# Prompt attention of a hybrid decoder step on one Trainium2 core: score tiles of up to 1024 keys cut into units of at most 512, and the setup's loads in another order

## What is computed

```python
def diff_attend(q, k, v, q_pos, k_pos, lam):
    s = jnp.einsum('ntkgch,nskch->nkgcts', q, k, preferred_element_type=jnp.float32) * SCALE
    mask = k_pos[None, :] <= q_pos[:, None]
    s = jnp.where(mask, s, -jnp.inf)
    p = jax.nn.softmax(s, axis=-1)
    a = p[:, :, :, 0] - lam * p[:, :, :, 1]
    return jnp.einsum('nkgts,nskv->ntkgv', a, v.astype(jnp.float32))
```

## Time and profile before

| | |
|---|---|
| median of the executions | 2490.93 us |
| the profiled execution | 2487.62 us, its span 2485.8 us |
| busy in the span | PE 87%, PEld 80%, DVE 46%, ACT 39%, POOL 51% |
| mean granted TensorE clock | 0.912 of full |
| setup, to the first instruction of the next block | 0 to 50.6 us |
| prompt attention | about 1482 to 2080 us |

### The profile page before, as it was taken

One profiled execution on the slowest core, in us unless ns is written; L12 is line 12 of the kernel. 1 busy time (PEld: TensorE's weight loads), 2 busy tenths in 40 slices (PEclk: granted clock), 3 DMA queues, 4 the chain that ended last, 5 costly groups with the idle time before them and its releaser, 6 DMA issues. The chain is left out here.

```text
span 2485.8 us, 37618 instructions
## 1 busy us (share of the span) xinstructions
PE 2170.9 (87%) x13193; PEld 1995.5 (80%) x13193; DVE 1155.8 (46%) x1914; ACT 971.2 (39%) x1572; POOL 1279.6 (51%) x682
## 2 busy tenths in 40 slices
PE   4999999999279998999889987877777787898998
PEld 4999999999279998999889985655665666666998
DVE  3698889889845003222100005555555554346101
ACT  4455555555444112111121125555555554234111
POOL 2799999999733324433311125555455552224232
PEclk7999999999669999999989987888888887997999
DMA  6112111121223222223222230000000005882221
GB/s 234 51 54 65 60 60 60 48 63 53 84 60 122 69 94 88 69 77 94 90 82 95 86 128 26 18 26 18 17 26 17 9 1 155 255 262 76 60 77 70
DMA packets 182037, 192.51 MB, mean 77 GB/s; under 512 B 11435, under 2 KB 147060, under 8 KB 181332
## 3 DMA queue, kind: packets, MB, share of 16 engines
q1 hardware_dynamic: 181952, 191.48, 24.4%
HBM read 145.52 MB, written 47.63 MB: 78 GB/s over the span
## 5 line engine op out<-in xcount | busy, mean ns | idle before, releaser
L222 POOL TENSOR_TENSOR w_lo<-w_raw,w_hi 128x1024 fp32r<-128x1024 f32 x116 | 279.6, 2411 | 603.3 <-ACT w_hi L218 603.3
L242 PE MATMUL ps<-Hhi,w_hi 128*128 128x352 f32 x1704 | 560.5, 329 | 18.3 <-POOL w_lo L222 11.7
L242 PE MATMUL ps<-Hhi,w_lo 128*128 128x352 f32 x1704 | 550.9, 323 | 0.0
L242 PE MATMUL ps<-Hlo,w_hi 128*128 128x352 f32 x1704 | 549.9, 323 | 0.0
L777 DVE SCALAR_TENSOR_TENSOR ps<-U,dww,ps 128x512 f32<-128x512 f32 x608 | 403.1, 748 | 0.0
L218 ACT ACTIVATE w_hi<-w_raw 128x1024 fp32r<-128x1024 f32 x116 | 122.1, 1053 | 665.7 <-PE ps L242 244.6
L696 POOL TENSOR_TENSOR pool_acc<-pool_acc,prod 128x1024 f32<-128x1024 f32 x144 | 346.3, 2405 | 31.0 <-ACT prod L645 22.7
L242 PEld LDWEIGHTS ps<-Hhi,w_hi 128*128 128x128 f32 x1704 | 321.9, 189 | 27.9 <-POOL w_lo L222 18.4
L242 PEld LDWEIGHTS ps<-Hlo,w_hi 128*128 128x128 f32 x1704 | 323.1, 190 | 2.1
L242 PEld LDWEIGHTS ps<-Hhi,w_lo 128*128 128x128 f32 x1704 | 322.1, 189 | 0.0
L645 ACT ACTIVATE prod<-U,dww 128x1024 f32<-128x1024 f32 x176 | 197.0, 1147 | 249.8 <-POOL pool_acc L696 143.3
(11 more groups left out here) (237 smaller groups left out, 3876.4 us busy)
## 6 DMA issues: line engine op xcount, KB each, us to landing
w_raw<-conv_w_in SPq DMA_DIRECT2D x48, 512.0 KB, 4.1
w_raw<-attn_w_in SPq DMA_DIRECT2D x40, 512.0 KB, 4.7
kpage<-cache_k SPq DMA_DIRECT2D x64, 256.0 KB, 3.0
vpage<-cache_v SPq DMA_DIRECT2D x64, 256.0 KB
res<-Y SPq DMA_DIRECT2D x2, 4224.0 KB, 21.4
gate<-sg SPq DMA_DIRECT2D x16, 528.0 KB, 4.0
sgl<-gate SPq DMA_DIRECT2D x16, 528.0 KB, 3.7
xres<-res SPq DMA_DIRECT2D x16, 528.0 KB, 3.9
```

What stands on the lines that cost most here:

```text
L222: pool.tensor_tensor(wlo[s][:, :, :], raw[s][:, :, :], whi[s][:, :, :].bitcast(F32), ALU.subtract).then_inc(w_lo, 1)
L242: mm = pe.matmul(ps[:, 3 * dst + c, 0:CH], w[:, k, :], r(k)[:, c * CH:(c + 1) * CH], start=start and k == 0 and w is whi[s] and r is rhs_h ...
```

## The change

Attention: the tiles with i >= 4 are cut into two units, one of 512 keys and one of the rest, so that a head has 12 units (4 narrow tiles, then 4 x 2) in place of 8 tiles. A unit never takes more than one bank for each softmax, the bank pairs alternate by unit, and the scores of unit u wait for the exps of unit u - 2. The two units of a wide tile have maxima of their own: the second unit's exps use the joint minimum of the negated maxima (`run_done`), ACT makes two weights that bring the first unit to the same maximum, DVE joins the sums, POOL scales three pieces and then adds. `LAG` goes from 2 tiles to 5 units; on DVE the maxes now stand ahead of the coefficients. Products of small statistics are written as reductions over adjacent columns of `stats`, with one operand, in place of `tensor_tensor`. `p0` gets eight buffers and `p1` four. `v_hi` moves from behind `hi` to ahead of it, `q_hi` from i = 4 to the unit with y % 12 = 1.

Setup: the weight tiles are loaded last of the small loads; `st_in` is loaded only when the norm's roots are made; the spreading of the norms comes ahead of `dwin` and lambda; the state is transposed in the next block, behind the first `unit_by_tile`; the wait for the write of `res` moves there too. Five semaphores cover the nine input loads.

```diff
     (setup, SP)
-                for s, kind in ((0, 0), (1, 1)):
-                    sp.dma_start(raw[s][:, :, :], conv_src(0, kind)).then_inc(raw_in[s], 16)
...
-                sp.dma_start(dwin[:, :], a["conv_dw_w"][0]).then_inc(dw_in, 16)
                 for i, name in enumerate(("attn_lambda_q1", "attn_lambda_k1", "attn_lambda_q2", "attn_lambda_k2")):
                     sp.dma_start(lamv[:, i, :], a[name]).then_inc(lam_in, 16)
+                sp.dma_start(dwin[:, :], a["conv_dw_w"][0]).then_inc(dw_in, 16)
                 sp.dma_start(ptab[:, :], a["page_table"].rearrange("(o b) p -> o (b p)", o=1)).then_inc(lam_in, 16)
-                sp.dma_start(stg[:, :, :], st_src).then_inc(st_loaded, 16)
-
+                for s, kind in ((0, 0), (1, 1)):
+                    sp.dma_start(raw[s][:, :, :], conv_src(0, kind)).then_inc(raw_in[s], 16)
                 sp.wait_ge(xe_act, NXT)
                 sp.wait_ge(xe_dve, NXT)
+                sp.wait_ge(Norm.std_ready, 1)
+                sp.dma_start(stg[:, :, :], st_src).then_inc(st_loaded, 16)
                 sp.dma_start(res_d[0], Y[:, :, :]).then_inc(res_out[0], 16)
-                sp.wait_ge(res_out[0], 16)
     (next block: PE; ACT and DVE copy the state out and wait for res_out)
+                        unit_by_tile(pe, n, e, e, norms[0])
+                        if first and s == 0:
+                            turn_state()
     (attention)
+        LAG = 5
+        UNITS = 12
+        VALUES = {10: (0, (0,)), 11: (0, (1, 2)), 12: (0, (3,)),
+                  17: (1, (0, 1)), 18: (1, (2, 3)), 19: (1, (4, 5)), 20: (1, (6, 7))}
+        OUTPUTS, TOTALS, SUMS = {13: 0, 21: 1}, {14: 0, 22: 1}, {15: 0, 23: 1}
+        NEW_VALUES, NEXT_Q = 9, 1
...
+        def score_ap(x, n, c):
+            return ps[:, 2 * (unit_of(x, n) % 2) + c, 0:width(x, n)]
     (PE scores)
+                    if u >= 2:
+                        pe.wait_ge(exp_done, 2 * NU * g + 2 * (u - 2) + 2)
     (ACT)
+                def exp(g, x, n, c):
+                    if n == 0:
+                        act.wait_ge(mx_done, 2 * NU * g + 2 * unit_of(x, n) + c + 1)
+                    else:
+                        act.wait_ge(run_done, 4 * GH * g + wides(x) + 1)
...
+                def weight(g, x):
+                    for c in range(2):
+                        act.activation(stat(x, N_E + 2 * c), stat(x, N_NM + 2 * c), ACT.Exp, scale=-1.0,
+                                       bias=stat(x, N_RUN + c)).then_inc(weight_done, 1)
+                def step(g, y, top):
+                    j = y // UNITS
+                    if y < top:
+                        x, n = tile_of(y)
+                        for c in range(2):
+                            exp(g, x, n, c)
+                        if n == 1:
+                            weight(g, x)
+                    if y == NU - 1 and top > NU:
+                        k_hi(g + 1)
+                    if y % NU == NEW_VALUES and y < top:
+                        v_hi(g + y // NU)
+                    if 0 <= y - LAG < top:
+                        hi(g, y - LAG)
+                    if y % UNITS == NEXT_Q and UNITS * (j + 1) < top:
+                        q_hi(g, j + 1)
+                    for h, half in due(y, top, OUTPUTS):
+                        output(g, h, half)
     (DVE)
+                def maxes(g, x, n):
...
+                    if n == 1:
+                        dve.wait_ge(mx_done, 2 * NU * g + 2 * u + 2)
+                        dve.tensor_reduce(stat(x, N_RUN, 2), stat_pairs(x, N_NM), AX.X, ALU.min).then_inc(run_done, 1)
+                def coefficients(g, x):
...
+                    if wide:
+                        dve.wait_ge(weight_done, 8 * GH * g + 2 * wides(x) + 2)
+                        step_up(dve.tensor_reduce(stat(x, N_ES, 2, 2), stat_pairs(x, N_E), AX.X, ALU.mult))
+                        step_done()
+                        step_up(dve.tensor_reduce(stat(x, N_S, 2, S_STEP), stat_pairs(x, N_ES), AX.X, ALU.add))
+                        step_done()
+                    dve.tensor_reduce(stat(x, N_T0), stat(x, N_S, 2), AX.X, ALU.mult).then_inc(rc_done, 1)
+                    dve.reciprocal(stat(x, N_R1), stat(x, N_S + S_STEP)).then_inc(rc_done, 1)
+                    if wide:
+                        dve.wait_ge(rc_done, 20 * GH * g + coefs(x) + 1)
+                        dve.tensor_reduce(stat(x, N_U), stat(x, N_E + 2, 2, N_T0 - N_E - 2), AX.X, ALU.mult
+                                          ).then_inc(rc_done, 1)
+                def step(g, y, top):
+                    if y < top:
+                        maxes(g, *tile_of(y))
+                    if 0 <= y - 1 < top and is_last(y - 1):
+                        coefficients(g, tile_of(y - 1)[0])
+                    if 0 <= y - LAG < top:
+                        lo(g, y - LAG)
     (POOL, wide tiles)
+                    if last:
+                        pool.tensor_scalar(b[:, 0:512], b[:, 0:512], stat(x, N_U), stat(x, N_R1),
+                                           ALU.mult, ALU.mult).then_inc(pn_done, 1)
+                        pool.tensor_scalar(a[:, 0:512], a[:, 0:512], stat(x, N_E), 1.0,
+                                           ALU.mult, ALU.mult).then_inc(pn_done, 1)
+                    pool.tensor_scalar(b[:, last:w], b[:, last:w], stat(x, N_T0), stat(x, N_R1),
+                                       ALU.mult, ALU.mult).then_inc(pn_done, 1)
+                    pool.wait_ge(pn_done, 16 * GH * g + x + 1 + 2 * wides(x + 1))
+                    pool.tensor_tensor(a[:, 0:w], a[:, 0:w], b[:, 0:w], ALU.add).then_inc(comb_done, 1)
```

More of the change, by code:

```diff
@@ L492, in _ @@
                                    ).then_inc(act_step.sem, act_step.up())
+                act.wait_ge(setup, 3)
+                act.wait_ge(act_step.sem, act_step.now())
+                act.activation(ncol[:, 0:QT], ncol[:, 0:QT], ACT.Sqrt, scale=1.0 / D, bias=eps_rms)
+                act.activation(ncol[0:NS_TOK, QT:NXT], ncol[0:NS_TOK, QT:NXT], ACT.Sqrt, scale=1.0 / D,
+                               bias=eps_rms[0:NS_TOK]).then_inc(Norm.std_ready, 1)
                 act.wait_ge(cols_turned, 1)
@@ L629, in _ @@
                         unit(pe, n + 2, e, e, h_hi, h_lo)
+                tiles(0, first=True)
+                with pe.Fori(1, JT // 2) as i:
+                    tiles(i)
                 pe.wait_ge(sg_done, JT)
@@ L639, in _ @@
                 norm_act(act, norms[0])
+                for m in range(0, JT // 2, 2):
+                    act.wait_ge(st_turned, m + 1)
+                    act.activation(state[:, 2 * m:2 * m + 2, :].rearrange("p j n -> p (j n)"), ps[:, 6, 0:4 * SR], ACT.Copy
+                                   ).then_inc(st_act, 1)
+                act.wait_ge(st_dve, JT // 4)
+                act.wait_ge(res_out[0], 16)
                 def products(i, s, part):
@@ new lines, in scores @@
+                    dst = [score_ap(x, n, c) for c in range(2)]
+                    masked = n == parts(x) - 1
+                    for m, (ql, kr) in enumerate(((qhi, khi), (qhi, klo), (qlo, khi))):
+                        for c in range(2):
+                            rows_ = slice(HD * c, HD * c + HD)
+                            mm = pe.matmul(dst[c], ql[s][rows_, i * P:(i + 1) * P], kr[rows_, 512 * n:512 * n + w],
+                                           start=m == 0, stop=m == 2 and not masked)
+                            if m == 2 and not masked:
+                                mm.then_inc(s_done, 1)
@@ L1602, in hi @@
                         act.wait_ge(pv_done, 2 * (GH * g + j - 1) + half + 1)
[L1603 to L1607 removed]
+                    act.wait_ge(tg_done, NU * g + tg + 1)
@@ L1609, in output @@
+                    act.activation(aThi[half][:, b0:b0 + nb, (i % 4) * P:(i % 4 + 1) * P],
+                                   ps[:, 4 + tg % 2, 0:nb * P].rearrange("p (b n) -> p b n", b=nb),
+                                   ACT.Copy).then_inc(hi_done, 1)
                 def output(g, j, half):
@@ L1675, in step @@
-                def step(g, x, top):
-                    j, i = divmod(x, QT)
-                    if 0 <= x - 1 < top:
-                        coefficient(g, x - 1)
-                    if x < top:
-                        maxes(g, x)
-                    if 0 <= x - LAG < top:
-                        lo(g, x - LAG)
-                    if x == NX - 1 and top > NX:
+                    tg, b0, nb = tgroups(x)[n]
+                    dve.wait_ge(hi_done, NU * g + tg + 1)
+                    cs = slice((i % 4) * P, (i % 4 + 1) * P)
@@ new lines, in lo, with step @@
+                    dve.tensor_tensor(aTlo[half][:, b0:b0 + nb, cs],
+                                      ps[:, 4 + tg % 2, 0:nb * P].rearrange("p (b n) -> p b n", b=nb),
+                                      aThi[half][:, b0:b0 + nb, cs].bitcast(F32), ALU.subtract
+                                      ).then_inc(lo_done, 1)
+                def step(g, y, top):
```

(21 more changed lines are left out.)

332 lines of the change are left out of this document (155 added, 177 removed).

## The result

The changed kernel takes **2595.28 us** (median of four executions, 2591.18 to 2598.86) against 2492.05 us for the kernel before on the same chip: a ratio of **1.0414**, 95% interval 1.0395 to 1.0433. It is slower, as forecast, but by 103 us and not by 33; the time lies 20 us beyond the range (2478 to 2575). The profiled execution took 2593.79 us, its span (first to last instruction) is 2591.9 us, its mean granted clock 0.888 against 0.912.

A forecast was written before the change was run, and what follows sets the result against it. Bound: the attention's circle of maxes, exps, high and low parts. Heads 32 us slower, `v_hi` +3.8, last tile +1, setup -4.3: +32.5 on 2487.6 gives 2520, plus 3.3 for the median: 2524 us, range 2478 to 2575.

The forecast's parts named there:

- the ring: Attention: maxes, exps, high part, low part, next maxes wait on each other in a circle, 36.8 us a head after the change.
- the ACT overload: At y % 12 = 1 ACT's next queries, copy and squares take 2.4 us against DVE's 1.8: +0.6 us a head.
- I take 0.7, near the low end, because the lead covers short bursts: PE's own addition to each attention head, from its compute speed at a lower clock: 0.7 us, bounds 0 and 3.2.
- +3.8: Attention: `v_hi`, moved ahead of `hi`, adds 0.95 us four times, 3.8 us in all.
- hidden by five units of lag: POOL's extra pieces in wide tiles, about 4.4 us a head, cost nothing except 1 us at the very last tile.
- group changes: 0: Attention, change of group: same chain of new keys, low part and scores as before, adding 0.
- Net -4.3: Setup: next block 9.6 us earlier, state's transposes paid again at about 5.3 us; net -4.3 us, bounds -10 and +5.
- PE's wait for the exps was the bound: Rival, chance 0.16: in the attention's wide tiles the 98 us of PE waits come back, giving 2424 us, or 2473 at half.
- The joint minimum waits for POOL: Rival, chance 0.08: DVE's joint minimum, 64 times in the attention, is delayed by POOL, +30 us, giving 2554 us.
- PE at 1.2 GHz and stays: Rival, chance 0.05: in the attention PE's clock drops to 1.2 GHz throughout, +144 us, giving 2668 us.
- The ring is cheaper: Rival, chance 0.10: attention with small operations of 0.1, no late PE, setup at -10, about 2490 to 2500 us.
- The 17 us of the two-operand product: DVE's coefficient product takes 283 ns against 150 unhindered, 17 us over 127; already inside the old head time, gone after.

The follow-up runs named there:

- e3: Changed kernel with POOL's low part of the new values ahead of the join and PE's `total` one unit later: 2523.12 us, ratio 1.0142 to the kernel before.
- e2: Changed kernel with only PE's sums over the squares (`total`) one unit later: 2550.56 us, ratio 1.0258 to the kernel before.
- e6: e3 with ACT's high part moved ahead of the two exps of its step: 2419.79 us, ratio 0.9721 to the kernel before.
- e1: Changed kernel with only POOL's low part of the new values put ahead of the join: 2568.17 us, ratio 1.0319 to the kernel before.
- e8: Kernel before with only its small statistics changed (one-operand reductions, squares once for eight tiles): 2498.14 us, ratio 1.0051.
- e10: e6 with DVE's loop over the first three groups written out: 2401.78 us, ratio 0.9645 to the kernel before.
- e11: e8 with DVE's loop over the groups written out: 2487.61 us, ratio 1.0001 to the kernel before.
- e13: Changed kernel with only DVE's loop over the groups written out: 2583.29 us, ratio 1.0390 to the kernel before.
- e4: Kernel before with only the setup's part of the change, attention unedited: 2480.46 us, ratio 0.9973.
- e9: e6 run again unchanged, the announced edit being absent: 2414.13 us, ratio 0.9709 to the kernel before.
- e7: Kernel before with only ACT's high part of tile x - 2 ahead of the exps of tile x: 2475.35 us, ratio 0.9955.

## Why the prediction was right and wrong

**The direction and the ring: right.** The sum gave the ring 36.8 us a head; e3, in whose plain heads no other wait of size is left, shows 37.0 in the head taken apart above and 36.8 to 37.8 in all. The pieces hold one by one. A second or first half of four blocks was 0.72 + 1.36 + 1.24 = 3.32 by the hand sum; in the changed kernel:

```profile
1751.92 1.28 DVE L1725 TENSOR_REDUCE stats<-ps 128x1 f32<-128x512 f32 x2
...
1754.61 0.69 DVE L1758 TENSOR_TENSOR aTlo<-ps,aThi 128x512 fp32r<-128x512 f32 x1 [1.28 <-ACT aThi L1663]
1755.22 0.48 DVE L1725 TENSOR_REDUCE stats<-ps 128x1 f32<-128x128 f32 x2
```

3.30. The 0.6 us for the ACT overload is there too, one unit behind where it was put (3.29 at y % 12 = 2, where 0.59 + 1.13 + 0.99 = 2.71 would do). The weights take 288 ns each, two in 0.47 with the overlap, against the 0.32 assumed for two; the joint minimum 157 ns.

**"I take 0.7, near the low end, because the lead covers short bursts": the step that failed, first.** This term for PE was put at 0.7 us a head and came to 3.5. It asked only how fast PE computes, with bounds of 0 and 3.2 us a head. It never asked what PE waits for. Each unit is shorter than a tile, PE runs up to two units ahead, and `total` stood one unit behind ACT's squares, which ACT makes at the end of its step; in the kernel before it stood one whole tile behind and waited 1.2 us in all. In a plain head the stall costs 5.22 - 3.29 at one unit and 4.27 - 2.58 at another, 3.6 us, and e2 gets 39 us back in all: in the traces 3.4 on average in the eleven heads that are not the first of a group, and 0 to 4 in the first heads, where PE's wait for `vlo` stays. A lower clock by itself is not what lengthens the head: in e3 the mean granted clock of the attention is 0.74 as well, and a plain head takes 37 us. Why it is 0.74 there, and 0.83 before and 0.82 in e6, no run takes apart.

**"+3.8" for `v_hi`, and "hidden by five units of lag" for POOL: the step that failed, second.** The 0.95 us a group are there: the unit y % 12 = 9 takes 4.91 us in the first head of a group and 3.96 in the others. But the prediction followed only ACT. Behind `v_hi` comes POOL's `v_lo`, behind a join, and the values' matmuls, one unit later where two tiles lay between, are the next thing on PE, with the scores of the following unit behind them. The prediction counted POOL's busy time (25 of 37 us; measured 382 of 690) and not its order. The first heads cost 42.5, 56.4, 56.4 and 49.6 against 40.5: 43 us over plain ones. In e1 they are 29.7 shorter, although PE still waits 23 us there; the 13 that stay are about the two jumps (2 x 5) and `v_hi` in the ring (3.8). The whole kernel gains only 24 by e1's ratio; in the profiled execution of e1 the attention begins 4.5 us later than in that of the changed kernel. The term "group changes: 0" holds: the last heads of the groups cost 3.6 us over a plain head, before 5.5.

**The jump: a term that the prediction does not have.** Two stands of 5.1 us of DVE. In the kernel before, DVE's loop jumps back twice as well, and the trace shows no `issue` line in the attention, so no row of before could give its price. What decides whether a jump costs is open: in the traces one turn of e8's loop has some 300 instruction rows on DVE and the stands are there, one of the kernel before has some 360 and they are not. The Trainium skill (Runtime: NRT & Kernel Launch, Instruction fetch mechanics) says that a taken branch to a target outside of the two pages held makes the engine wait for a fetch; runs e10, e11 and e13, in which the stands go with the jump, agree, but none shows pages.

**The setup: right in kind.** "About 41" was 39.4, "some 5.3" for the transposes 5.2. "Net -4.3" is inside e4's interval of -11 to -2, whose centre is -7. Two misses work against each other in it: ACT's last square ended near 23 and not at 20.9, and `dwin` was there before 29.4, earlier than the 30.5 worked out from its 16 GB/s.

**Why e3 lands on the forecast.** Forecast 2524, e3 2523; over the kernel before of its own batch (2487.86) e3 is 35 us slower, the forecast 33. That is partly luck: a plain head is 0.5 us shorter than the 37.5 forecast (-8 us) and the setup some 3 to 7 us better, while the two jumps (+10) and the four remaining waits for `vlo` (23 us of idle PE, some of it covered) go the other way.

**What would show it.** The signs set down were mixed and would have told: DVE's largest wait is for `aThi`, small reductions take 0.15, `nh` starts near 41; but PE's wait for exps is down to a third and not nearly gone, heads take over 40 us and not 37 to 38, and DVE's waits for PE's scores, fewer than before, are up to 11.2 us long, before 4.6. That last line leads to what PE waits for.

**The rivals.** *PE's wait for the exps was the bound* (0.16): out. That wait fell by two thirds and the time rose. Its condition was slack in the ring; e6 makes the slack and there a gain comes, 2420. That this is near the 2424 worked out for the rival confirms nothing: e6 also takes the two stalls out and the high parts out of the ring, which that sum does not hold. *The joint minimum waits for POOL* (0.08): out, 157 ns each. *PE at 1.2 GHz and stays* (0.05): out; a mean of 0.74 says that about half of the time was spent at each level. *The ring is cheaper* (0.10): out, 37.0. *The 17 us of the two-operand product*: they were rightly left out of the sum. The rows show the product shorter (283 to 146 ns), and in e11 that buys nothing that can be measured. That it stood beside the exps, and so cost nothing, is argued and not shown. The Trainium skill (SBUF — State Buffer, Who interferes with whom) says that on trn2 `tensor_reduce` does not contend with GpSimd. The changed kernel agrees: its small reductions took 142 to 163 ns, while the product with two operands took 149 to 1192 ns before.

## What to carry to other kernels

When work is cut finer, walk through every wait of every engine with the new step lengths, above all the waits of the engine that runs ahead: a consumer one step behind its producer was safe with a step of 4.4 us and is not with one of 3.1 (plain heads of 35.4 us in 8 steps, of 37.0 in 12). Follow an operand to its last maker and look at what stands in front of it in that maker's queue, not at how busy the maker is. And if a ring of waits closes once per step, cutting steps finer makes it close more often; change the order along with it so that it no longer closes (here one line, the high part ahead of the exps, with enough lag behind it: 4.2% with the units, 0.45% without). The version e10 does all of it and takes 0.9645 of the time of the kernel before.

## What the runs showed of the hardware

- DVE idled 4.5 to 5.1 us at each jump back of its loop in the changed kernel, e1, e2, e3, e6, e9 and e8, with nothing in the profile that it waited for, and not in the kernel before, e4 and e7; with the loop written out (e10 to e13) the idle time is gone.
- 128 small products at 146 ns in place of 283 bought nothing: ratio 1.0001 (0.9987 to 1.0015), with DVE's loop written out (e11).
- Behind a wait of PE of 3.01 us the granted clock was 0.50 for some 6 us of full work. Yet e3, without these waits, has the same mean of 0.74, so what they cost through the clock is not shown.
- An exp over one column takes 288 ns, two of them back to back 0.47 us; four small reductions and a reciprocal in a row on DVE take 0.7 us.
